# A fused two-block fp32 network on one core: rounded weights first, the remainder's pass last, in every three-pass tile

## The reference

```python
def reference(x, ...):
    x = first_block(x, ...)      # 2 layers: mixer (four head groups), then an FFN with a causal convolution
    return second_block(x, ...)  # 272 tokens (16 meta tokens ahead): FFN, mixer, FFN in each layer

def swiglu(x, w_in, w_out):
    g, u = jnp.split(x @ w_in, 2, axis=-1)
    return (jax.nn.silu(g) * u) @ w_out

for layer in range(DEPTH):       # second_block
    h = h + (0.5 * swiglu(rms_norm_2(h, ffn1_norm[layer]), ffn1_w_in[layer], ffn1_w_out[layer])).astype(h.dtype)
    hn = rms_norm_2(h, mix_norm[layer])
    # layer 0: even_mixer (sparse attention and retention); layer 1: odd_mixer (window attention and pooling)
    ...
    h = h + (0.5 * swiglu(rms_norm_2(h, ffn2_norm[layer]), ffn2_w_in[layer], ffn2_w_out[layer])).astype(h.dtype)
return h[:, N_META:]
```

## Time and profile before

| | us |
|---|---|
| median of 3 timed runs | 1837.28 |
| lowest, highest | 1834.20, 1838.16 |
| the profiled execution | 1837.04 |
| its span in the trace | 1835.3 |
| TensorE busy | 1810.9 (99%) |
| VectorE busy | 1173.9 (64%) |
| ScalarE busy | 797.1 (43%) |
| mean granted clock of TensorE | 0.995 |

### The profile page before, as it was taken

One profiled execution on the slowest core, in us unless ns is written; L12 is line 12 of the kernel. 1 busy time (PEld: TensorE's weight loads), 2 busy tenths in 40 slices (PEclk: granted clock), 3 DMA queues, 4 the chain that ended last, 5 costly groups with the idle time before them and its releaser, 6 DMA issues.

```text
span 1835.3 us, 32584 instructions
## 1 busy us (share of the span) xinstructions
PE 1810.9 (99%) x13296; PEld 1706.6 (93%) x13296; DVE 1173.9 (64%) x1855; ACT 797.1 (43%) x1058; POOL 36.0 (2%) x19
## 2 busy tenths in 40 slices
PE   9999999999999999999999999999999999999999
PEld 7888999969899999999988888999999999889999
DVE  6766887457588856665447632677556764547763
ACT  3556555245465544343245342434344332424442
POOL 0000000000000000000051000000000000000000
PEclk9999999999999999999989999999999999999999
DMA  5332555424145554555332422455545453144553
GB/s 199 116 115 92 184 183 212 164 96 176 57 149 179 202 213 153 179 190 193 111 126 105 161 103 78 157 170 205 186 144 175 171 208 121 65 171 164 188 219 117
DMA packets 35865, 284.31 MB, mean 155 GB/s; under 512 B 4800, under 2 KB 6976, under 8 KB 8256
## 3 DMA queue, kind: packets, MB, share of 16 engines
q1 hardware_dynamic: 35776, 283.05, 43.2%
HBM read 281.98 MB, written 1.05 MB: 154 GB/s over the span
## 4 chain that ended last, share of the span: by engine, by line
PE 86%; DVE 8%; ACT 4%; issue 1%; DMA 1%; POOL 0%; ACTq 0%; DVEq 0%; SPq 0%
PE PS L1313 22%; PE PS L1314 21%; PE PS L1315 21%; PE PS L821 3%; PE PS L1214 2%; PE PS L670 2%; PE PS L693 2%; DVE split L1996 2%; PE PS L793 2%; PE PS L1256 2%; PE PS L716 1%; PE PS L736 1%; PE PS L995 1%; DVE W L2621 1%; DVE split L1993 1%
## 5 line engine op out<-in xcount | busy, mean ns | idle before, releaser
L1313 PE MATMUL PS<-Hhi,split 128*128 128x272 f32 (+1 forms) x2176 | 623.0, 286 | 8.7 <-DVE split L1996 3.3
L1314 PE MATMUL PS<-Hlo,split 128*128 128x256 f32 (+1 forms) x2080 | 591.2, 284 | 0.0
L1315 PE MATMUL PS<-Hhi,split 128*128 128x256 f32 (+1 forms) x2080 | 589.4, 283 | 0.0
L1996 DVE TENSOR_TENSOR split<-wa,split 128x2048 fp32r<-128x2048 f32 (+2 forms) x174 | 358.5, 2060 | 125.9 <-ACT split L1439 125.9
L1313 PEld LDWEIGHTS PS<-Hhi,split 128*128 128x128 f32 x2176 | 411.9, 189 | 15.5 <-issue 6.6
L1314 PEld LDWEIGHTS PS<-Hlo,split 128*128 128x128 f32 x2080 | 390.7, 188 | 0.2
L1315 PEld LDWEIGHTS PS<-Hhi,split 128*128 128x128 f32 x2080 | 390.9, 188 | 0.0
L1439 ACT CAST split<-wa 128x2048 fp32r<-128x2048 f32 (+2 forms) x174 | 299.2, 1720 | 63.4 <-PE PS L1315 63.4
L1313 PE MATMUL PS<-hidhi,split 128*128 128x256 f32 (+1 forms) x1088 | 309.6, 285 | 0.6 <-DVE hidlo L2633 0.6
L1315 PE MATMUL PS<-hidhi,split 128*128 128x256 f32 (+1 forms) x1088 | 309.0, 284 | 0.0
L1314 PE MATMUL PS<-hidlo,split 128*128 128x256 f32 (+1 forms) x1088 | 308.0, 283 | 0.0
(11 more groups left out here) (344 smaller groups left out, 2485.4 us busy)
## 6 DMA issues: line engine op xcount, KB each, us to landing
wa<-in_wfi SPq DMA_DIRECT2D x126, 1024.0 KB, 4.8
wa<-in_wfo SPq DMA_DIRECT2D x48, 1408.0 KB, 6.0
wa<-in_wmix SPq DMA_DIRECT2D x26, 2048.0 KB, 7.8
wa<-in_wmix SPq DMA_DIRECT2D x4, 1536.0 KB, 6.4
H<-in_wfi SPq DMA_DIRECT2D x3, 1024.0 KB, 9.8
G<-in_wfi SPq DMA_DIRECT2D x3, 1024.0 KB, 4.8
wa<-in_wmix SPq DMA_DIRECT2D x2, 1024.0 KB, 5.3
wa<-in_wmix SPq DMA_DIRECT2D x2, 768.0 KB, 7.4
```

Of the source, the lines that this page charges most:

```text
L1313: pe.matmul(o, hi, xhi, start=first, stop=False)
L1314: pe.matmul(o, hi, xlo, start=False, stop=False)
L1315: return pe.matmul(o, lo, xhi, start=False, stop=last)
L1996: dve.tensor_tensor(out=wlo[n % 2][:, at:width], in0=wa[:, c % 2, at:width], in1=whi[n % 2][:, at:width].bitcast(F32), op=ALU.subtract).th ...
```

## The change

`product3` is cut in two. `rounded` issues the two passes with the rounded weight, `remainder` the third. A tile or pair now runs `rounded` over all its k tiles, waits for the remainder (mx_lo, ev_rest or ev_lo, head_lo or w_lo) and runs `remainder` over all its k tiles; ahead of the first pass it waits only for the rounded weights (mx_hi, ev_hi, head_hi or w_hi). In the even mixer the fourth "rq" tile moves ahead of the first scores, and every later filling tile up to the first "v0" moves one place ahead of the small steps; ScalarE's and VectorE's orders follow. The programs of GpSimd and SyncE are as before. The core of the diff:

```diff
-            def product3(o, hi, lo, xhi, xlo, first, last):
+            def rounded(o, hi, xhi, xlo, first):
                 pe.matmul(o, hi, xhi, start=first, stop=False)
                 pe.matmul(o, hi, xlo, start=False, stop=False)
+            def remainder(o, lo, xhi, last):
                 return pe.matmul(o, lo, xhi, start=False, stop=last)
...
@@ pair
-                    split_wait = isinstance(i, int) and i == 0 and r in headed(f)
-                    if split_wait:
-                        pe.wait_ge(S.head_lo, heads + headed(f).index(r) + 1)
+                    head = isinstance(i, int) and i == 0 and r in headed(f)
+                    turn = heads + headed(f).index(r) + 1 if head else 0
+                    if head:
+                        pe.wait_ge(S.head_hi, turn)
                     else:
-                        pe.wait_ge(S.w_lo, i + (n + r + 1))
+                        pe.wait_ge(S.w_hi, i + (n + r + 1))
                     pe.wait_ge(S.act_done, i + (acts[0] + r - 3))
...
+                        if head and k == KD // 2:
+                            pe.wait_ge(S.w_hi, n + r + 1)
+                        for j in range(2):
+                            rounded(PS[:, 2 * r + j, 0:T], hi[:, k, P * j:P * j + P], xhi[:, k, 0:T], xlo[:, k, 0:T], k == 0)
+                    if head:
+                        pe.wait_ge(S.head_lo, turn)
+                    else:
+                        pe.wait_ge(S.w_lo, i + (n + r + 1))
+                    for k in range(KD):
+                        if head and k == KD // 2:
                             pe.wait_ge(S.w_lo, n + r + 1)
                         for j in range(2):
-                            mm = product3(PS[:, 2 * r + j, 0:T], ...)
+                            mm = remainder(PS[:, 2 * r + j, 0:T], lo[:, k, P * j:P * j + P], xhi[:, k, 0:T], k == KD - 1)
@@ output tiles
-                        pe.wait_ge(S.head_lo, 4 * i + (heads + len(headed(f)) + r + 1))
+                        pe.wait_ge(S.head_hi, 4 * i + (heads + len(headed(f)) + r + 1))
...
                             if r == 0 and k == KF - 2:
                                 pe.wait_ge(S.act_done, acts[0])
                             if k == KF // 2:
+                                pe.wait_ge(S.w_hi, 4 * i + (n + KF + r + 1))
+                            rounded(PS[:, 4 + r, 0:T], hi[:, k, :], hidhi[:, k, 0:T], hidlo[:, k, 0:T], k == 0)
+                        pe.wait_ge(S.head_lo, 4 * i + (heads + len(headed(f)) + r + 1))
+                        for k in range(KF):
+                            if k == KF // 2:
                                 pe.wait_ge(S.w_lo, 4 * i + (n + KF + r + 1))
-                            mm = product3(PS[:, 4 + r, 0:T], ...)
+                            mm = remainder(PS[:, 4 + r, 0:T], lo[:, k, :], hidhi[:, k, 0:T], k == KF - 1)
@@ even mixer, TensorE
                 mean_square(k)
                 fill("rq", w)
                 fill("rq", w)
+                fill("rq", w)
                 pe.wait_ge(S.nr_done, upto(S.nr_done, 2))
                 pe.wait_ge(S.dv_out, 3)
                 for a in dsa:
                     attend_scores(a, 0)
-                fill("rq", w)
+                w = slot(6)
+                fill("rk", w)
                 for a in dsa:
                     attend_transposes(a, 0)
-                w = slot(6)
                 fill("rk", w)
...
```

More of the change, by code:

```diff
@@ L783, in split_column @@
                         pe.wait_ge(S.mx_xlo, l + 1)
+                    pe.wait_ge(S.mx_hi, pieces + n + 1)
+                    for k in range(KD):
+                        rounded(places[SEQ][:, place, :], hi[:, k, :], Xhi[:, k, :], Xlo[:, k, :], k == 0)
                     pe.wait_ge(S.mx_lo, pieces + n + 1)
                     for k in range(KD):
-                        mm = product3(places[SEQ][:, place, :], hi[:, k, :], lo[:, k, :], Xhi[:, k, :], Xlo[:, k, :], k == 0,
-                                      k == KD - 1)
+                        mm = remainder(places[SEQ][:, place, :], lo[:, k, :], Xhi[:, k, :], k == KD - 1)
                     mm.then_inc(S.mx_used, 1)
@@ L1009, in split_tile @@
                     i = n % 4
+                    hi = piece_hi[n % 3].rearrange("p (k c) -> p k c", k=KD)
+                    lo = wa_lo[:, w, KD * P * i:KD * P * (i + 1)].rearrange("p (k c) -> p k c", k=KD)
+                    if ks[0] == 0:
+                        pe.wait_ge(S.ev_hi, n + 1)
+                    for k in ks:
+                        rounded(PS[:, bank, 0:TT], hi[:, k, :], Ehi[:, k, :], Elo[:, k, :], k == 0)
                     if ks[0] == 0:
@@ L1159, in even @@
                     attend_transposes(a, 1)
-                fill("rk", w)
+                w = slot(7)
+                fill("v0", w)
                 for a in dsa:
@@ L1163, in even @@
                     attend_scores(a, 2)
-                w = slot(7)
-                for _ in range(3):
+                for _ in range(2):
                     fill("v0", w)
@@ L1736, in even @@
                 round_piece(17)
+                filled_tile("rq")
+                round_piece(18)
                 for a in dsa:
                     attend_exp(a, 0)
[L1739 to L1742, removed]
                 filled_tile("rk")
@@ L1745, in even @@
                 for a in dsa:
+                    attend_copies(a, 0)
+                filled_tile("rk")
+                round_piece(20)
+                for a in dsa:
                     attend_exp(a, 1)
                 filled_tile("rk")
-                round_piece(20)
-                filled_tile("rk")
                 round_piece(21)
-                for a in dsa:
-                    attend_copies(a, 1)
                 filled_tile("rk")
@@ L1755, in even @@
                 for a in dsa:
+                    attend_copies(a, 1)
+                filled_tile("v0")
+                round_piece(23)
+                for a in dsa:
                     attend_exp(a, 2)
-                for n in range(23, 26):
+                for n in range(24, 26):
                     filled_tile("v0")
@@ L2448, in even @@
                     attend_max(a, 1)
+                rest_piece(19)
                 for a in dsa:
                     attend_divide(a, 1)
-                for n in range(19, 22):
+                for n in range(20, 22):
                     rest_piece(n)
```

7 lines of the change are left out of this document (1 added, 6 removed).

## The result

| | us, median | lowest, highest |
|---|---|---|
| before (8 runs) | 1836.34 | 1834.19, 1838.61 |
| after (8 runs) | 1840.51 | 1836.38, 1844.09 |

The ratio is 1.0021, with a 95% interval of 1.0012 to 1.0030. In a second study with 11 runs of after against 29 of before it was 1.0015 (1.0006 to 1.0025). By the two ratios after is slower by about 3 to 4 us; the differences of the medians are 4.2 and 2.4 us. The forecast, 1831.2, had the wrong sign, and 1840.51 lies outside its own range of 1827 to 1835.

The account below looks back on a forecast made before the run. The prediction took TensorE's matmul cadence as the bound (busy 1810.9 of 1835.3 us). Its terms, +1.6 (FFNs) - 2.4 - 5.0 = -5.8, took 1837.04 to 1831.2 us, own range 1827 to 1835, wider range 1825 to 1841.

Parts of the forecast that it names:

- Pairs, -12.2: FFN pairs: remainder waits at pair starts go, 8.5 us in FFN1 and 2, 2.5 in FFN3 to 5, 1.2 in FFN6.
- Rival (c): FFN1 and 2 pairs: the small stalls have another cause than the remainder and stay, 1839.7 us; chance 0.08.
- First output tile, +13.8: Each FFN's first output tile: waits ahead of k = 20 with less work in front, 3 x 2.36 + 3 x 2.23 us.
- Rival (e): First output tiles: the waits ahead of k = 20 don't come, as VectorE is sooner, 1817.4 us; chance 0.05.
- Even mixer, -2.4 and -5.0: Even mixer: earlier start on ev_hi, -2.4 us; scores' idle and low clock go, net -5.0 us.
- its new waits: Even mixer, behind the scores: new idle of 0.75 us at the first transposes and 0.4 for the next scores.
- Rival (d): Even mixer: the moved rq tile only moves the wait; softmax late or later tiles wait, 1834.6 us; chance 0.10.
- Cadence, 0: All FFN matmuls: the new order of passes leaves the time per matmul unchanged, 0 us.
- The bound of +9.5: FFNs' 9504 matmuls: one ns more for each would add 9.5 us.
- rival (b): FFN matmuls: the new order of passes is slower by 1 ns each, 1840.7 us; chance 0.15.
- Clock in the new waits, 0: First output tiles: granted clock stays 1.00 behind all six waits ahead of k = 20, costing 0 us.
- rival (a): First output tiles: clock falls in the waits ahead of k = 20, 3.4 us each, 1838.0 to 1851.6; chance 0.22.

Follow-up runs that it names:

- the control: Changed kernel with the loop over the output tiles' two halves written out and no surplus matmuls: 1840.61 us.
- the late: Changed kernel, but each FFN's first output tile runs both passes over its first 20 k tiles (60 matmuls) before waiting for the last hidden tile: 1820.95 us.
- the filled: Changed kernel, output-tile loop written out, with 20 (256 tokens) or 16 (272) surplus matmuls ahead of the wait for the last hidden tile: 1835.59 us.
- the partly filled wait: Changed kernel, output-tile loop written out, with only 8 (256 tokens) or 6 (272) surplus matmuls ahead of the last hidden tile's wait: 1835.07 us.
- the last version: Against before: even mixer as changed, pairs await the remainder behind 20 of 48 matmuls, output tiles and first mixer as before: 1818.58 us, ratio 0.9906.

## Why the prediction was wrong

Taken by its own steps, two of them failed, the clock in the new waits and the cadence:

- **Pairs, -12.2: right.** FFN1 won 116.27 - 112.80 = 3.5 us, 4.0 with the cadence's 20 x 0.027 taken out; FFN2 3.8, or 4.3 of the 4.5. The single stalls of FFN3 to FFN6 went. Rival (c) is dead.
- **First output tile, +13.8: right.** 10.69 - 8.36 = 2.33 in FFN1, 10.50 - 8.24 = 2.26 in FFN3, 10.21 - 7.87 = 2.34 in FFN6, so 3 x 2.33 + 3 x 2.26 = 13.8. Rival (e) is dead.
- **Even mixer, -2.4 and -5.0: right** (-7.4 measured for it alone), though its new waits were smaller and so part of the match is luck. More than half of the gain is low clock (17.1 us of it in before's trace, 6.8 in that of the even mixer alone), and before's own low stretch behind the scores isn't in every execution: the trace of the run with the order of passes alone has the same wait of 2.8 us and no fall behind it. Nor is the wait for GpSimd always 2.7 us; it is 3.5 to 3.7 in the three other traces with the even mixer's old wait (the FFNs alone, the order of passes alone, the rq tile alone). Rival (d) came true only without the tile's late wait.
- **Cadence, 0: wrong in size.** "I take 0, since the order of k and of operands already differs between these two shapes": but those differences say nothing of a sequence that no row shows. A pair takes 0.027 us more at 256 columns and 0.020 at 272, an output tile of 256 columns 0.04 more: 66 x 0.027 + 66 x 0.020 + 24 x 0.04 = +4.1 us, an estimate from the traces. The bound of +9.5 held it. This is rival (b) at under half its price. The kernel with that order alone shows the slower pair, and in its time 1.5 us.
- **Clock in the new waits, 0: this is the step that failed.** The forecast had granted clock 1.00 behind all six waits and gave rival (a) 0.22, as a thing that happens or not. It happens in about half of the waits, in changing ones. In the four traces with the six waits open (the changed kernel twice, the control, the FFNs alone) there are 12 falls in 24 waits and 47.8 us of low clock, so per execution 47.8/4/2 = 6 us; filling the waits wholly or in part gave 4.9 to 5.5 us back. None is in the traces of the late, the filled or the partly filled wait. The price of one fall was wrong as well: half of the low time was right, but ten of the twelve stretches last 3.4 us and not 6.8, so a fall cost 2 us on average and not 3.4.

The sum by these: -5.8 + 4.1 + 6 = +4.3, where +4.2 and +2.4 were measured. That it meets the first to 0.1 us is luck: for the FFNs alone the same terms give -12.2 + 13.8 + 4.1 + 6 = +11.7, and +9.6 was measured (8.3 to 13.0 by the interval).

The prediction set 2.1 to 2.8 us of idle against 1.06 and 0.92, which brought no fall, and against 2.83, which did. What decides stands between these, and none of its rows lay there; the nearest that before has is a wait of 1.5 us (L693, at 24 us), with no low clock behind it. The traces show a gradation, though of few cases: of the eight waits of 2.9 us (start to start) six brought a fall, of the four of 2.4 us two, of the twelve of 2.25 us four. The rule that the prediction cites (the Trainium skill, TensorE: Matmul & The Clock Gate, HAM oscillation — how this bites in real kernels) would have had no fall in any of the six; the runs speak against it as it stands, with falls behind waits of 2.25 us.

That the change lost 3 to 4 us and did not win 5.8 is thus due to two costs that each look like nothing in one profile: 0.5% of a pair, and a clock that falls in some executions.

## What to carry to other kernels

When a loop is cut in two so that a late operand is awaited later, look for every other wait that sat late in the old loop: it now stands in the first part, with all of the second part behind it. Here the mend is to run the k tiles that are ready through both parts first, and it was worth 19 us. In a kernel whose TensorE is 99% busy, price an idle time at its length plus the fall that may follow, and take that as an expected value over executions, not from one trace.

## What the runs showed of the hardware

- The same waits of 2.25 to 2.9 us (start to start) brought low clock in 12 of 24 cases, ten times for 3.4 and twice for 6.8 us; it began between 0.7 us ahead of the restart and 1.6 us behind it. In the one trace of the partly filled wait 1.94 us brought none in two cases and 1.5 us none in four; nine of its runs lie at 1834.2 to 1836.9, so this seems to hold in most executions. Two waits of 1.8 and 2.1 us, start to start, in the trace of the rq tile alone brought none either.
- The even mixer's old wait for QK, 2.8 us of idle, was followed by low clock in two of three traces, for 6.8 and 3.4 us.
- The low stretch at the even mixer's start, which begins among or just behind matmuls of 8 columns, is in all thirteen traces: 10.2 us long in two, 6.8 in nine and 3.4 in two (the partly filled one and the last version).
- The time of a run of the changed kernel follows its mean granted clock: its first eight go from 1836.38 at 0.997 to 1844.09 at 0.993.
- The same 48 matmuls take 5.613 us with the three passes interleaved, 5.640 with the remainder's pass apart, and 5.63 with the first five of eight k tiles apart; the cause of this was not sought.
